# A two-layer trunk on one core: small steps of the mixers moved, one copy laid out anew, and the end split by token halves

## The reference

```python
a = jnp.where(strict, jnp.einsum('bhnld,bhnsd->bhnls', k_beta, k) * decay, 0.0)
sol = lax.linalg.triangular_solve(a, rhs, left_side=True, lower=True, unit_diagonal=True)
...
x = x + _swiglu(h, *ffn[layer])      # after layer 1: return _rmsnorm(x, final_norm)
```

## Time and profile before

| | |
|---|---|
| median of 3 runs | 2778.9 us (2778.72 to 2780.67) |
| profiled execution | 2782.74 us, its span 2780.9 us |
| PE busy | 2749.2 us, 99% |
| DVE, ACT busy | 1550.4 us (56%), 1418.4 us (51%) |
| POOL busy | 86.0 us (3%) |
| granted TensorE clock, mean | 0.997 |
| read from HBM | 503.91 MB, 183 GB/s over the span |

### The profile page before, as it was taken

The page is one execution under the profiler, slowest core; times in us unless marked ns, Lnnn a source line. Parts: engine busy times, 40 slices in busy tenths (PEclk is TensorE's granted clock), DMA queues, the critical chain, the costliest instruction groups (busy, mean ns, idle before and its releaser), DMA issues.

```text
span 2780.9 us, 37152 instructions
## 1 busy us (share of the span) xinstructions
PE 2749.2 (99%) x13558; PEld 2288.9 (82%) x13558; DVE 1550.4 (56%) x1939; ACT 1418.4 (51%) x2005; POOL 86.0 (3%) x79
## 2 busy tenths in 40 slices
PE   9999999999999999999999999999999999999998
PEld 7878888888888888887888887887888888888886
DVE  5544665545455444457686868655545444454444
ACT  5444555444444444458787877544444444444443
POOL 0000000000000000001111111000000000000000
PEclk9999999999999999999999999999999999999999
DMA  7564466666666666656465646555666666666664
GB/s 256 152 190 145 155 195 187 193 186 188 190 189 190 188 192 190 190 171 188 152 184 157 185 157 202 170 174 179 186 195 189 189 188 189 188 189 190 209 193 150
DMA packets 263889, 510.97 MB, mean 184 GB/s; under 512 B 20416, under 2 KB 20672, under 8 KB 263504
## 3 DMA queue, kind: packets, MB, share of 16 engines
q1 hardware_dynamic: 259792, 494.54, 59.5%
q0 software_dynamic: 3152, 11.57, 1.4%
q10 hardware_dynamic: 816, 3.15, 0.3%
HBM read 503.91 MB, written 5.28 MB: 183 GB/s over the span
## 4 chain that ended last, share of the span: by engine, by line
PE 91%; DVE 5%; ACT 2%; issue 1%; DVEq 1%; DMA 0%; ACTq 0%; SPq 0%
PE acc L583 28%; PE acc L589 28%; PE acc L584 28%; DVE wlo L1476 2%; PE aux L636 2%; PE aux L810 2%; DVE arena L1913 1%; DVE arena L1910 1%; PE aux L816 1%; DVE arena L1872 0%; DVEq L1912 0%; PE aux L804 0%; PE aux L796 0%; ACT arena L1331 0%; DVE arena L1889 0%
## 5 line engine op out<-in xcount | busy, mean ns | idle before, releaser
L1476 DVE TENSOR_TENSOR wlo<-wraw,whi 128x1024 fp32r<-128x1024 f32 x928 | 1145.5, 1242 | 1006.6 <-ACT whi L1005 1004.6
L1005 ACT ACTIVATE whi<-wraw 128x1024 fp32r<-128x1024 f32 x928 | 978.2, 1060 | 1132.9 <-PE acc L589 1069.0
L583 PE MATMUL acc<-whi,hT_hi 128*128 128x512 f32 x2624 | 1037.1, 395 | 1.8 <-ACT whi L1005 1.3
L584 PE MATMUL acc<-whi,hT_lo 128*128 128x512 f32 x2624 | 1023.9, 390 | 0.0
L589 PE MATMUL acc<-wlo,hT_hi 128*128 128x512 f32 x2624 | 704.4, 390 | 6.8 <-DVE wlo L1476 6.6
L589 PEld LDWEIGHTS acc<-wlo,hT_hi 128*128 128x128 f32 x2624 | 492.0, 188 | 114.1 <-DVE wlo L1476 11.7
L583 PEld LDWEIGHTS acc<-whi,hT_hi 128*128 128x128 f32 x2624 | 494.2, 188 | 103.3 <-ACT whi L1005 1.7
L584 PEld LDWEIGHTS acc<-whi,hT_lo 128*128 128x128 f32 x2624 | 494.4, 188 | 99.4
L583 PE MATMUL acc<-whi,arena 128*128 128x512 f32 x1088 | 425.1, 391 | 3.2 <-ACT whi L1005 3.2
L584 PE MATMUL acc<-whi,arena 128*128 128x512 f32 x1088 | 424.1, 390 | 0.0
L589 PE MATMUL acc<-wlo,arena 128*128 128x512 f32 x1088 | 291.4, 390 | 0.0
(11 more groups left out here) (254 smaller groups left out, 1193.8 us busy)
## 6 DMA issues: line engine op xcount, KB each, us to landing
wraw<-in_l_w_in SPq DMA_DIRECT2D x304, 512.0 KB, 4.3
wraw<-in_l_w_gate SPq DMA_DIRECT2D x176, 512.0 KB, 3.7
wraw<-in_l_w_up SPq DMA_DIRECT2D x176, 512.0 KB, 3.7
wraw<-in_l_w_down SPq DMA_DIRECT2D x176, 512.0 KB, 4.4
wraw<-in_l_w_out SPq DMA_DIRECT2D x96, 512.0 KB, 4.6
arena<-decay_sums POOLq DMA_DIRECT2D x16, 512.0 KB, 5.3
o_rounds<-arena POOLq DMA_DIRECT2D x3, 1024.0 KB, 5.3
arena<-o_rounds ACTq DMA_DIRECT2D x3, 1024.0 KB, 5.9
```

Source lines behind the costliest of these rows:

```text
L583: nc.tensor.matmul(pair[m], hi[:, k, tok], wh, start=first, stop=False)
L584: nc.tensor.matmul(pair[m], lo[:, k, tok], wh, start=False, stop=False)
L1005: nc.scalar.activation(whi[:, s, :], wraw[:, s, :], ACT.Copy).then_inc(hi_done, 1)
L1476: V.tensor_tensor(wlo[:, s, :], wraw[:, s, :], whi[:, s, :].bitcast(F32), ALU.subtract).then_inc(lo_done, 1)
```

## The change

1. `L0_SLOTS`: the step that turns q and k of layer 0's mLSTM, from slot 17 to 20, on all engines.
2. Gate chain of layer 1: gate transposes behind unit 9 (was 10), the sums behind 14 (16), DVE's parts at 12, 13, 18 (12, 14, 19), ACT's at 13, 17 (13, 18).
3. `EA_AT`: in round 0 the decay exponentials at s = 1, 2 (3, 4).
4. `diag` is laid out [blocks, column] instead of [column, blocks], so that ACT's copy has an inner run of 32 elements on both sides, and DVE's transpose reads it with a stride of 32. The unit matrix is copied at s = 9, ahead of the diagonal; so is the wait for the stored output of the round before.
5. Round 0's output is loaded at s = 2 of round 3 (was 10). z gates 0 and 1 at units 142 and 154 (146, 151). `z_out(2)` at unit 5 of its block (3).
6. Out1's transposes of the last round behind PE's unit 4 (7), DVE's split at 8 (9).
7. The last block: its first 18 units as before; the last four for tokens 0 to 127, all four, and then for 128 to 255. Each half has its own add, gain, squares, mean, root, reciprocal and scaling; ACT scales the first 512 columns, DVE the others; SP stores eight pieces of 256 KB.

```diff
-L0_SLOTS = ([0, 3, 5, 7, 9, 16, 17, 33, 35, 37, 39, 41, 43, 45, 47]
+L0_SLOTS = ([0, 3, 5, 7, 9, 16, 20, 33, 35, 37, 39, 41, 43, 45, 47]
...
-Z_GATED = [146, 151, 164, 167, 173, 181, 189]
+Z_GATED = [142, 154, 164, 167, 173, 181, 189]
...
-EA_AT = lambda r, c: (3, 4)[c] if r == 0 else (-3, -2)[c]
+EA_AT = lambda r, c: (1, 2)[c] if r == 0 else (-3, -2)[c]
...
-        diag = at(90 * KB, [P, LEAF, M * HV])
+        diag = at(90 * KB, [P, M * HV, LEAF])
...
-            half = lambda n: slice(n * D // 2, (n + 1) * D // 2)
-            for n in range(2):
-                for m in range(M):
-                    sp.wait_ge(epi_step[m], n + 1)
-                    sp.dma_start(out[m * P:(m + 1) * P, half(n)], x[:, m, half(n)]).then_inc(out_done, 16)
+            for m in range(M):
+                for n in (1, 0, 2, 3):
+                    sp.wait_ge(epi_step[m][n], 1)
+                    sp.dma_start(out[m * P:(m + 1) * P, n * NB:(n + 1) * NB], x[:, m, n * NB:(n + 1) * NB]).then_inc(out_done, 16)
...
+            def last_gemm_block(name, hi, lo):
...
+                for m in range(M):
+                    tok = slice(m * P, (m + 1) * P)
+                    for j in range(upb - SLOTS, upb):
+                        n, slot = units_done(j)
+                        pe.wait_ge(hi_done, n)
+                        for kk in range(2):
+                            wh = whi[:, slot, kk * NB:(kk + 1) * NB]
+                            nc.tensor.matmul(acc[1][:, m, :], hi[:, 2 * j + kk, tok], wh, start=False, stop=False)
+                            nc.tensor.matmul(acc[1][:, m, :], lo[:, 2 * j + kk, tok], wh, start=False, stop=False)
+                        pe.wait_ge(lo_done, n)
+                        for kk in range(2):
+                            mm = nc.tensor.matmul(acc[1][:, m, :], hi[:, 2 * j + kk, tok], wlo[:, slot, kk * NB:(kk + 1) * NB],
+                                                  start=False, stop=j == upb - 1 and kk == 1)
+                    mm.then_inc(half_done, 1)
...
-                if w == GATES_AT + 4:
+                if w == GATES_AT + 3:
                     gate_transposes(1)
-                if w == GATES_AT + 10:
+                if w == GATES_AT + 8:
                     gdn_gates()
...
-                if w == 7:
+                if w == 4:
                     o_transposes(3)
...
                     silu(K)
+                    if r == ROUNDS - 1:
+                        act.wait_ge(conv_tr, TOK_AT(r, V0))
+                        load_o(0)
...
+                if s == 9:
+                    if r:
+                        act.wait_ge(o_stored, 16 * r)
+                    nc.scalar.activation(flat(leaf_t[:]), C["leaf_eye"], ACT.Copy)
                 if s == 10:
                     act.wait_ge(a_set, D_AT(r, 1))
-                    if r:
-                        act.wait_ge(o_stored, 16 * r)
                     for b in range(4):
-                        nc.scalar.activation(diag[quarter(b), :, :],
-                                             A_[quarter(b), :, :, quarter(b)].rearrange("p c h j -> p j (c h)"), ACT.Copy)
-                    nc.scalar.activation(flat(leaf_t[:]), C["leaf_eye"], ACT.Copy).then_inc(diag_set, 1)
-                    if r == ROUNDS - 1:
-                        act.wait_ge(conv_tr, TOK_AT(r, V0))
-                        load_o(0)
+                        a = nc.scalar.activation(diag[quarter(b), :, :],
+                                                 A_[quarter(b), :, :, quarter(b)].rearrange("p c h j -> p (c h) j"), ACT.Copy)
+                    a.then_inc(diag_set, 1)
...
-                if w in (GATES_AT + 7, GATES_AT + 12):
+                if w in (GATES_AT + 7, GATES_AT + 11):
...
-                if j == (5 if b in (Z_BLOCK + 2, Z_BLOCK + 4) else 3) and b > Z_BLOCK:
+                if j == (5 if b in (Z_BLOCK + 2, Z_BLOCK + 3, Z_BLOCK + 4) else 3) and b > Z_BLOCK:
...
+            for m in range(M):
+                act.wait_ge(last_added, m + 1)
+                nc.scalar.activation(aux[1][:, m * NB:(m + 1) * NB], xs[:, m, :], ACT.Square, accum_out=ssq[:, m, 3:4]
+                                     ).then_inc(last_squares, 1)
+                act.wait_ge(last_mean, m + 1)
+                nc.scalar.activation(rms[:, m:m + 1], mean[:, m:m + 1], ACT.Sqrt, bias=epsc[:, 0:1], scale=1.0 / D).then_inc(last_rms, 1)
+                act.wait_ge(last_rstd, m + 1)
+                nc.scalar.activation(x[:, m, 0:NB], x[:, m, 0:NB], ACT.Copy, scale=rstd[:, m:m + 1]).then_inc(epi_step[m][0], 1)
...
                     V.transpose(lead[:].rearrange("p j i -> p (j i)"),
-                                diag[:].unsqueeze(2).to_broadcast([P, LEAF, 2, LEAF // 2]))
+                                diag[:].rearrange("p k j -> p j k").unsqueeze(2).to_broadcast([P, LEAF, 2, LEAF // 2]))
...
-                if w in (GATES_AT + 6, GATES_AT + 8, GATES_AT + 13):
+                if w in (GATES_AT + 6, GATES_AT + 7, GATES_AT + 12):
...
-                if j == 9:
+                if j == 8:
                     o_split(3)
...
+            for m in range(M):
+                dve.wait_ge(half_done, m + 1)
+                V.tensor_tensor(xs[:, m, :], acc[1][:, m, :], x[:, m, 3 * NB:], ALU.add).then_inc(last_added, 1)
+                dve.drain()
+                V.tensor_tensor(x[:, m, 3 * NB:], xs[:, m, :], fgain[:, 3 * NB:], ALU.mult)
+                dve.wait_ge(last_squares, m + 1)
+                V.tensor_reduce(mean[:, m:m + 1], ssq[:, m, :], AX.X, ALU.add).then_inc(last_mean, 1)
+                dve.wait_ge(last_rms, m + 1)
+                V.reciprocal(rstd[:, m:m + 1], rms[:, m:m + 1]).then_inc(last_rstd, 1)
+                dve.drain()
+                for n in range(1, 4):
+                    V.tensor_scalar(x[:, m, n * NB:(n + 1) * NB], x[:, m, n * NB:(n + 1) * NB], rstd[:, m:m + 1], None, ALU.mult
+                                    ).then_inc(epi_step[m][n], 1)
```

More of the change, by code:

```diff
@@ L373, in build @@
         o_lo = sem("o_lo")
-        epi_step = [sem(f"epi_step{m}") for m in range(M)]
+        half_done = sem("half_done")
+        last_added = sem("last_added")
+        last_squares = sem("last_squares")
+        last_mean = sem("last_mean")
+        last_rms = sem("last_rms")
+        last_rstd = sem("last_rstd")
+        epi_step = [[sem(f"epi_step{m}_{n}") for n in range(4)] for m in range(M)]
         l1_const = sem("l1_const")
@@ L496, in _ @@
             phase("dn1", 2, 1, 2, down1)
-            half = lambda n: slice(n * D // 2, (n + 1) * D // 2)
-            for n in range(2):
-                for m in range(M):
-                    sp.wait_ge(epi_step[m], n + 1)
-                    sp.dma_start(out[m * P:(m + 1) * P, half(n)], x[:, m, half(n)]).then_inc(out_done, 16)
-            sp.wait_ge(out_done, 16 * 2 * M)
+            for m in range(M):
+                for n in (1, 0, 2, 3):
+                    sp.wait_ge(epi_step[m][n], 1)
+                    sp.dma_start(out[m * P:(m + 1) * P, n * NB:(n + 1) * NB], x[:, m, n * NB:(n + 1) * NB]).then_inc(out_done, 16)
+            sp.wait_ge(out_done, 16 * 4 * M)
         @block.gpsimd
@@ L660, in residual_phase @@
                 body(name, 0, 2, hi, lo, [last_f, xt(0, 1)], between=between, tiles=tiles)
+                if not transposed:
+                    gemm_block(name, UNIT_END - 2 * UPB[name], BLOCK_END // 2 - 1, hi, lo, 0, 0)
+                    last_gemm_block(name, hi, lo)
+                    return
                 with pe.Fori(1, 2) as i:
                     body(name, i, 2, hi, lo, [xt(i, 0), xt(i, 1)], tiles=tiles)
-                if transposed:
-                    pe.wait_ge(xlo_done, done + 4 + 3)
+                pe.wait_ge(xlo_done, done + 4 + 3)
             def last_x_block(name):
@@ L1452, in _ @@
             nc.scalar.activation(gate_t[:, 9, 0:1], epsc[:, 0:1], ACT.Sqrt)
-            last_x_block("dn1")
-            root(4)
-            act.wait_ge(x_gained, 4)
-            for n in range(2):
-                nc.scalar.activation(x[:, 1, n * D // 2:(n + 1) * D // 2], x[:, 1, n * D // 2:(n + 1) * D // 2], ACT.Copy, scale=rstd[:, 1:2]
-                                     ).then_inc(epi_step[1], 1)
+            act.drain()
+            act.wait_ge(x_gained, 1)
+            for m in range(M):
[6 more added lines that the diff above has]
+                nc.scalar.activation(x[:, m, 0:NB], x[:, m, 0:NB], ACT.Copy, scale=rstd[:, m:m + 1]).then_inc(epi_step[m][0], 1)
         @block.vector
@@ L2048, in _ @@
             last_f = ffn("gu1", "out1", last_x_block, FF // NB)
-            last_x_block = residual_phase("dn1", last_f)
-            last_x_block(1)
-            dve.drain()
-            V.tensor_tensor(x[:, :, 3 * NB:], xs[:], fgain[:, 3 * NB:].unsqueeze(1).to_broadcast([P, M, NB]), ALU.mult).then_inc(x_gained, 1)
-            last_x_block(3)
-            last_x_block(4)
-            for n in range(2):
```

(7 more changed lines are left out.)

13 lines of the change are left out of this document (added).

## The result

The changed kernel takes 2762.71 us (median of 5 runs, 2762.11 to 2763.5) against 2778.9 (5 runs, 2777.87 to 2780.67): ratio 0.9941, 95% interval 0.9926 to 0.9955. It is 16.2 us faster; 21.4 were forecast. Its profiled execution is the median one, 2762.71 us with a span of 2760.9; the kernel before has a span of 2780.9 in its profile. So the profiled pair differs by 20.0 us and the medians by 16.2, and both gaps to the forecast need an answer: 1.4 us within the pair, 3.8 between pair and medians.

What follows compares the result with a forecast made beforehand. TensorE, busy 2749.2 of 2780.9 us, was taken as the bound, leaving 13 us of stalls, 5 of slow clock and an 11 us tail. Terms summed to 21.4 us: 2761.3 profiled, 2757.5 as median, range 2751 to 2765.

Steps and rivals of the forecast that it cites:

- gate chain, round 0: Layer 1, units 28 to 30: earlier masks and exponentials end 2.55 us idle; gain 2.9 us (0.5 to 3.3).
- leaf of round 0: Layer 1: layout lead plus earlier exponentials end a 1.9 us stall and 1.7 of slow clock; gain 3.6 (0 to 3.6).
- round 3: Layer 1, units 154 and 156: moved z gates leave idle 1.5 and 1.7 us; gain 1.1 us (0 to 4).
- end: Last four units by token halves: earlier first output, only 1 MB left behind the matmuls; gain 4.1 us (2 to 4.8).
- tight place at L842: Round 0's second convolution ends at 1264.3, PE wants its buffer at 1264.7; costs tenths of a us if missed.
- Same DMA time: Round 0's gate chain: with unchanged DMA time the masks are ready at 1254, otherwise as early as 1251.
- lead of 1.85 us: Leaf of each round: faster diagonal copies and earlier unit matrix, less the slower transpose, start VectorE 1.85 us earlier.
- Rival (a): Whole kernel: the slow clock isn't given back, so gain 16.3 us, time 2762.6; chance 0.17.
- (b): VectorE stays the leaf's bound if its transpose takes over 3 us; rounds 0 and 3 keep stalls, 2763; chance 0.12.
- (c): Round 3's remaining stalls go too, with the transpose at 1.25 us; 2755 us; chance 0.08.
- (d): Slower: the strided transpose stalls PE once a round, turning the sign from 7.9 us on; 2787 at 10 us; chance 0.02.
- (e): The moved steps wait at their new places; only two tight places likely, under 1 us together; chance 0.03.

Runs made afterwards that it cites:

- end-alone run: The kernel before with only the last block's end done by token halves; 2775.23 us, 3.1 lower (0.9988).
- layout-alone run: The kernel before with only the diagonal's new layout and the unit matrix and stored-output wait one slot ahead; 2776.59 us, 1.8 lower (0.999).
- before again: The kernel before, unchanged, timed again; 2778.11 us over 11 runs, ratio 1.0001.
- q/k alone: The kernel before with only layer 0's q/k turning moved from unit 17 to unit 20; 2775.08 us, 2.9 lower (0.9987).
- Out1 alone: The kernel before with only the last round's Out1 transposes behind unit 4 and VectorE's split at 8; 2772.88 us, 5.5 lower (0.9983).
- chain back: The changed kernel with the gate chain and round 0's decay exponentials back at their old units; 2763.64 us, 0.9 over the changed kernel.
- gate-chain-alone run: The kernel before with only the gate chain moved up and round 0's decay exponentials two units earlier; 2775.73 us, 2.6 lower (0.9989).
- The last experiment: The kernel before with round 0's row copies of the decay sums loaded from an input, not behind the store; 2777.2 us, 0.75 lower (0.9995).

## Why the prediction was right, and where it missed

The direction, the parts and their order of size came out. By part, forecast, profiled pair (starts of PE's units in the two traces), and medians of the runs with one part alone:

| part | forecast | pair | alone |
|---|---|---|---|
| q/k later | 3.9 | 4.1 | 2.9 |
| gate chain, round 0 | 2.9 | 2.6 | 2.6 with the leaf |
| leaf of round 0 | 3.6 | 3.8 | 1.8 with rounds 1 to 3 |
| rounds 1 and 2 | 0.9 | 0.8 | |
| round 3 | 1.1 | 0.8 | not run |
| Out1's transposes | 4.9 | 5.0 | 5.5 |
| end | 4.1 | 2.8 | 3.1 |
| sum | 21.4 | 19.9 | 15.8 |

The five single parts sum to 15.8 us against 16.2 for the whole. That is no proof that they add up: each is known to 2.5 us, two of them remove the same stall, and round 3's gates are not among them.

**q/k, Out1.** Right in the pair: both stalls and the slow clock behind them are gone, and nothing took their place.

**Gate chain.** The mechanism is right, with the tight place at L842 missed by 0.7 us. "Same DMA time" held as a sum: from the store's issue to ready masks are 17.2 us in both traces (1242.80 to 1260.00 and 1233.07 to 1250.27), though split otherwise, 3.08 us before and 5.36 after from store to loads, and the masks themselves shorter. What failed is the start of the sum for the tight place: it set out from 1252.0, when ScalarE is free, and not from the masks, which the prediction's own slower case has ready at 1254. PE is 4.2 us earlier here, so on the prediction's clock the masks are ready at 1254.5, ScalarE starts at 1253.5 (behind the first of the two), and the convolution ends at 1265.4 instead of 1264.3. Putting the second exponential a unit later only moves the wait.

**Diagonal copies.** Copies 0.63 each and transpose 2.06 (2.06 to 2.10 over the four rounds) are the forecast's 2.55 for four and 2.1. The strided read costs VectorE per element about what the strided write did. But the term 3.6 is not the layout's: the chain alone cuts that stall to 0.3, and the old layout put back costs nothing. The prediction named both sources of the lead and did not ask whether one would do. The same holds for the 0.9 of rounds 1 and 2, which stay free of waits with the old layout. That the leaf's term came out in the pair (3.8) is right for a stall that ended, and no support for the lead of 1.85 us from the layout.

**Round 3.** Right: two waits for `wlo` of 1.4 each where 1.5 and 1.7 were forecast. The run with other z gates shows that these waits came from where the small pieces lie and are no bound of VectorE: two gates and one copy of z elsewhere take them from 2.8 to 0.5. Which of the three moves did it was not run.

**End.** The step that failed in size: "2.6 us at that rate". The first output is issued 2.8 us behind the last matmul, 2.5 were forecast; but the output then flows from 2756.3 to 2760.06, 3.8 us for 1 MB. The kernel before moved 410 to 426 GB/s in each microsecond from 2775 to 2779 and 389 in its last; the changed one is full at 363 to 373 and ends in a microsecond at 47 (rows above). Two things show in the queue's rows. The pieces of 512 columns go in packets of half the size: 578 packets carry 1.05 MB, where 576 carried 2.10, and they take the 16 engines 2.9 us (41.6% of 7), where 2.10 MB took 5.1 (73.2%), so 0.35 us more for 1 MB. The rest of the 1.2 us is the last, nearly empty microsecond. Together with the 0.3 of the later issue this makes, to a tenth, the 1.3 that are missing. Pieces of another shape were not run.

**Pair against medians.** The prediction said: "it lies 3.8 above the median 2778.9, and I carry the difference over". This is the step that failed: the changed kernel's profiled run is its own median, so the difference belonged to one long execution and not to the profiler. The median is 5.2 us above the forecast of 2757.5, of which this step is 3.8 and the end 1.3. Rival (a) gave 2762.6, and the median is 2762.71; that is partly luck, for its account, that the slow clock is not given back, is half of the cause at most. The profiles show two things that fell together in that one execution.

The first is the landing of the decay sums. Before, from the profile ahead, and in the end-alone run, whose code up to the last four units is the same:

```profile
1242.80 0.71 POOL L565 DMA_DIRECT2D decay_sums<-arena  x1 [53.45 <-ACT gate_t L1249]
1245.88 1.09 POOL L522 DMA_DIRECT2D arena<-decay_sums  x2 [2.37 <-DMA decay_sums<-arena]
```

```profile
1242.35 0.71 POOL L570 DMA_DIRECT2D decay_sums<-arena  x1 [53.43 <-ACT gate_t L1287]
1244.59 1.08 POOL L527 DMA_DIRECT2D arena<-decay_sums  x2 [1.53 <-DMA decay_sums<-arena]
1251.48 2.14 POOL L530 TENSOR_SCALAR_AFFINE_SELECT arena<-arena 128x1024 f32<-128x1024 f32 x2 [5.81 <-DMA arena<-decay_sums]
```

The store is followed by the loads after 3.08 us in one, 2.24 in the other, and the masks begin 10.7 or 6.9 us behind the loads' issue. The table of stretches of the end-alone run, and of the layout-alone run, which had the late landing (3.15):

```profile
160.00:170.00 10.00, 7.78 (x36) 6.62 (x35) 5.10 (x14) 3.82 (x5) 0.00 (x0) 0.83 0.35 107
1270.00:1290.00 20.00, 20.00 (x93) 16.45 (x92) 14.50 (x36) 19.45 (x30) 3.57 (x2) 1.00 0.47 150
```

```profile
160.00:170.00 10.00, 7.78 (x43) 6.45 (x42) 6.07 (x19) 5.04 (x6) 0.00 (x0) 1.00 0.33 104
1270.00:1290.00 20.00, 17.53 (x79) 13.65 (x78) 14.45 (x34) 18.77 (x35) 3.57 (x2) 1.00 0.54 168
```

With the late landing PE loses some 2.5 us in these two, with the early one nothing. Of seven profiles with the old chain and the store in its place, four were late (2.83 to 3.16 us from store to loads: before, before again, layout alone, q/k alone) and three early (2.24 in all: Out1 alone, end alone, chain back); PE is idle for 1.7 to 2.6 us in this stretch in the four, for 0.1 or less in the three. SyncE's weight loads around it were issued at the same distances from the store, within 0.05 us, in all of them; what makes the landing late stays open.

The second is the clock. Where a gap is untouched, it has the same length in every profile (but for the leaf's, 1.45 us in the run with rows from an input), yet not the same spell at 1.2 GHz behind it: layer 0's 2.2 us gap had it in 4 of 7 profiles (the two fences above show it with, 0.83, and without, 1.00, at the same 7.78 us busy), the leaf's 1.9 us gap in 2 of 6, Out1's 3.15 us gap in 6 of 7 (round 3's 1.85 us gap in 1 of 8, the gate-chain-alone run). At 1.7 us each that is 3.0 us on average, and the profile before had all three, 5.1. Layer 0's 2.2 + 4/7 x 1.7 = 3.2 lies near the measured 2.9, though the interval of that run would hold 2.2 or 3.9 as well. The changed kernel and its variants have none there in six profiles.

PE's units in the end-alone run, whose profiled execution is a median one, are 4.9 us earlier than in the profile before just ahead of the changed end: 3.3 from units 28 to 31, 1.2 from the clock at the leaf, 0.4 from further ahead. That is about the 4.7 us by which the profiled span (2780.9) lies over the median span of the kernel before (2776.2). So the long execution that the profile shows is accounted for. How often the timed runs have each of the two is not shown. The shares above come from profiled executions, which were the longest of their 11 in four cases of seven, so they are likely too high: a late landing costs 3.3 us, and of the 85 timed runs of the kernel before only 16 lie over 2780, not four in seven. The last experiment puts the landing's share in the median at 0.75 us, with an interval that holds nothing at all.

The rival of the leaf's bound (b) falls with the transpose at 2.1; (c) falls as round 3 kept its 2.8 us; (d) never came near; of (e) there is the 0.7 us at L842, within the "under 1 us together" that it gave.

## What to carry to other kernels

A profile is one execution, here often a long one: compare its span with the spans of the timed runs first. Before its stalls are summed, ask which of them end in something that varies (a round trip through memory, a clock spell behind a gap), and value those at how often they come, for a profile of the same code in another variant may not show them. When two edits feed the same stall, price them together, and undo each in the changed kernel: run alone, each looks worth its place. With TensorE at 99% the remaining gains are in where the small moved pieces land: two gates and a copy at other units gave 3.1 us, where a new layout gave none with the old places and some 0.6 with the new ones.

## What the runs showed of the hardware

- A strided fp32 read costs 1.65 to 1.85 times the contiguous one on both engines: ScalarE 1.16 against 0.63 us for 32x512, VectorE's transpose of 128x1024 2.06 to 2.10 against 1.25. The Trainium skill, "SBUF — State Buffer", section "Door 1: The DMA port swizzle", says that each access that crosses to a new 16-byte line pays a penalty; both engines' numbers agree.
- The same idle gap on TensorE is followed by a spell at 1.2 GHz in one execution and by none in another (gaps of 2.2, 1.9 and 3.15 us: 4 of 7, 2 of 6, 6 of 7 profiles). The Trainium skill, "TensorE: Matmul & The Clock Gate", section "Part 1: The HAM clock gate (the "warmup" mystery)", says that the judging window is not tied to the kernel's start; these counts agree. Without the gaps the spread is smaller too: 1.4 us over the 5 spans of the changed kernel (2760.3 to 2761.7), 4.9 over 11 of the kernel before (2775.5 to 2780.4), which have the late landings as well.
- GpSimd's two row masks of round 0 took 2.14 us where VectorE was in its convolution and 3.40 to 4.42 where they began beside the subtracts of `wlo`. One mask took 1.08 to 1.10 us wherever no such subtract ran beside it (141 of the 224 in all traces), and up to 3.40 where one did; many of those took no longer.
- Output pieces of 512 columns (2 KB a row) went at 363 to 373 GB/s with the 16 DMA engines full, those of 1024 columns at 410 to 426.
